# Finishing the output tiles from sums without the last two expert blocks

## What is computed

```
x = x + hier_moe(rmsnorm(x, norm2_g), w_rg, b_rg, w_re, b_re, w_gate, w_up, w_down)
y = rmsnorm(x, norm_f_g)

def hier_moe(x, ...):              # top-1 of 4 groups, then top-2 of the 4 experts in it
    for e in range(N_EXPERTS):     # 16 experts, d_model 1024, d_expert 512
        hid = jax.nn.silu(x @ w_gate[e]) * (x @ w_up[e])
        y = y + gates[..., e:e + 1] * (hid @ w_down[e])
```

## Time and profile before

| | |
|---|---|
| median of three runs | 938.05 us (937.69, 938.05, 940.88) |
| span of the profiled execution | 939.7 us, 1.65 us above the median; the page gives no other time for that execution |
| TensorE busy | 880.8 us, 94% |
| VectorE, ScalarE, GpSimd busy | 431.1, 154.5, 374.6 us |
| expert stage (first block's matmuls to the last's) | 534 to 908 us, 16 blocks |
| tail behind the last matmul | 908 to 939.7 us |
| granted clock of TensorE, mean | 0.976 |
| DMA | 163.15 MB, mean 174 GB/s, in the expert stage 291 to 360 GB/s a slice |

### The profile page before, as it was taken

One profiled execution on the slowest core, in us unless ns is written; L12 is line 12 of the kernel. 1 busy time (PEld: TensorE's weight loads), 2 busy tenths in 40 slices (PEclk: granted clock), 3 DMA queues, 4 the chain that ended last, 5 costly groups with the idle time before them and its releaser, 6 DMA issues.

```text
span 939.7 us, 16689 instructions
## 1 busy us (share of the span) xinstructions
PE 880.8 (94%) x6339; PEld 755.1 (80%) x6339; DVE 431.1 (46%) x1166; ACT 154.5 (16%) x456; POOL 374.6 (40%) x576
## 2 busy tenths in 40 slices
PE   5989999999999999999989799999999999999960
PEld 3974987869588695886945699999999999999920
DVE  3144474645646456463557843333333333333264
ACT  2031212121311213111131210000000000000071
POOL 4040031210302103021150258767767776777524
PEclk9989999999999999999999899999999999999985
DMA  9930203030110301003027389999999999999883
GB/s 328 280 151 1 68 1 80 12 79 1 28 52 1 79 1 34 25 1 57 1 62 291 71 294 299 327 352 335 360 346 333 327 322 326 315 319 314 248 305 115
DMA packets 90039, 163.15 MB, mean 174 GB/s; under 512 B 48887, under 2 KB 59027, under 8 KB 81770
## 3 DMA queue, kind: packets, MB, share of 16 engines
q1 hardware_dynamic: 70062, 136.43, 41.5%
q0 software_dynamic: 17728, 25.28, 11.2%
q10 hardware_dynamic: 2188, 0.59, 0.3%
HBM read 139.83 MB, written 25.87 MB: 176 GB/s over the span
## 4 chain that ended last, share of the span: by engine, by line
PE 51%; DMA 16%; issue 11%; POOL 11%; DVE 9%; ACT 1%; POOLq 1%; DVEq 0%; SPq 0%; ACTq 0%
PE bank L1527 48%; DMA z_d<-wout,win 12%; POOL z_d L599 7%; DVE wout L1443 2%; POOL wout L551 2%; PE bank L1532 1%; DVE wout L1436 1%; DVE win L1482 1%; DMA wout<-h_d,idt 1%; DMA h2T<-z_d 1%; DVE win L1407 1%; PE bank L1732 0%; DMA xbuf<-in_x_prompt 0%; POOL pad L595 0%; PE bank L1645 0%
## 5 line engine op out<-in xcount | busy, mean ns | idle before, releaser
L1527 PE MATMUL bank<-wout,win 128*128 128x150 f32 (+3 forms) x2048 | 246.3, 282 | 1.1 <-DVE wout L1129 1.1
L1527 PEld LDWEIGHTS bank<-wout,win 128*128 128x128 f32 x2048 | 244.7, 190 | 1.2 <-DVE wout L1129 1.2
L1527 PE MATMUL bank<-hT,win 128*128 128x128 f32 (+1 forms) x1536 | 182.9, 279 | 0.0
L1527 PEld LDWEIGHTS bank<-hT,win 128*128 128x128 f32 x1536 | 178.6, 192 | 1.5 <-issue 1.2
L1527 PE MATMUL bank<-win 128*128 128x130 f32 (+5 forms) x1024 | 137.3, 294 | 2.7 <-DVE win L1428 1.4
L599 POOL DMA_INDIRECT z_d<-wout,win x75 | 125.2, 1669 | 27.1 <-issue 26.8
L1527 PEld LDWEIGHTS bank<-win 128*128 128x128 f32 (+2 forms) x1024 | 125.5, 191 | 12.3 <-issue 10.3
L1527 PE MATMUL bank<-win,hT 128*128 128x260 f32 (+3 forms) x512 | 122.2, 417 | 3.0 <-DVE xbuf L1247 1.5
L1527 PE MATMUL bank<-wout,mixT 128*128 128x512 f32 (+1 forms) x384 | 116.8, 487 | 1.8 <-ACT mixT L845 1.7
L1527 PEld LDWEIGHTS bank<-win,hT 128*128 128x128 f32 (+1 forms) x512 | 77.1, 173 | 43.0 <-issue 34.1
L1436 DVE STREAM_TRANSPOSE wout<-bank 128x480 f32<-128x480 f32 (+1 forms) x45 | 25.1, 603 | 156.7 <-DMA z_d<-wout,win 155.2
(11 more groups left out here) (308 smaller groups left out, 812.0 us busy)
## 6 DMA issues: line engine op xcount, KB each, us to landing
win<-in_w_gate SPq DMA_DIRECT2D x32, 1024.0 KB, 6.3
win<-in_w_up SPq DMA_DIRECT2D x32, 1024.0 KB, 9.2
win<-in_w_down SPq DMA_DIRECT2D x32, 1024.0 KB, 10.6
win<-in_w_in SPq DMA_DIRECT2D x4, 2048.0 KB, 20.1
xbuf<-in_x_prompt SPq DMA_DIRECT2D x8, 512.0 KB, 3.8
wout<-in_w_out SPq DMA_DIRECT2D x1, 4096.0 KB, 15.6
z_d<-xbuf SPq DMA_DIRECT2D x32, 128.0 KB
h_d<-xn SPq DMA_DIRECT2D x8, 512.0 KB, 2.7
```

The lines of the kernel that those rows point to most:

```text
L1527: return nc.tensor.matmul(out, lhsT, rhs, start=first, stop=last)
```

## The change

The experts of positions 2 and 3 of the order (the smallest two beside experts 0 and 1) now get the last two positions, with blocks of 125 rows; the others move up. The kernel then finishes in this way:
- All nine tiles are read from `z_d` when the adds of block `sooner + 1` have landed, so their sums lack the last two blocks. Four tiles are read between the two halves of the last block's gate and up weights, five behind the second half. They are squared, normed and stored by SyncE.
- The adds of block `sooner + 2` still go to `z_d`, but wait until all nine tiles have been read (`sums_read`).
- Then the rows of both last blocks are read from `z_d` by two gathers of 125 rows (`fb`). Rows of the second last block need only the norm. Rows of the last block get its result added first. Both are written by indirect DMAs over the tiles, when these have landed.
- A row in both of the last blocks belongs to the last one. To leave it out of the other list, VectorE compares each id of the second last block with all ids of the last one (`lid`, loaded to all partitions), before it starts on block `sooner + 2`, and `away` moves such a row out of bounds.
- `products` of the last block stand behind the norms of both groups on VectorE, its silu behind all squares on ScalarE with a table load on either side. The last block's result has 8 products of 125 rows by 512 columns. `SHARED` is gone, the tiles `yb` lie in other buffers, and the gain `nfg` is loaded before block 3's weights.

```diff
-    SLOTS = ((30, 1), (30, 1), (26, 6), (27, 2), (28, 2), (30, 2))
+    SLOTS = ((30, 1), (30, 1), (26, 4), (27, 2), (28, 2), (30, 2))
     NS = sum(n for _, n in SLOTS)
-    SIZES = [NP * r for r, n in SLOTS for _ in range(n)] + [BLOCK] * (NE - NS)
+    LR, FX = 25, NE - 2
+    SIZES = [NP * r for r, n in SLOTS for _ in range(n)] + [BLOCK] * (FX - NS) + [NP * LR] * 2
...
+        order = sb("order", [P, NE])
...
+            after(sp, "stores", 16 * 8)
+            sp.dma_start(nfg, norm_f_g.rearrange("(a d) -> a d", a=1).broadcast_to([P, D])).then_inc(nf_in, 16)
             after(sp, "table_ready", 1)
             nblocks = sp.value_load(tabi[0:1, 2 * (NB + 1):2 * (NB + 1) + 1], min_val=NE, max_val=NB)
             sooner = sp.value_load(tabi[0:1, 2 * (NB + 1) + 1:2 * (NB + 1) + 2], min_val=NE - 3, max_val=NB - 3)
-            with sp.Fori(3, nblocks + 1) as j:
+            with sp.Fori(3, nblocks) as j:
...
+            def fetch_sums(t):
+                sp.dma_start(xa[t][0:ROWS[t], :], z_d[START[t]:START[t] + ROWS[t], :]).then_inc(z_rows[t], 16)
+            e = sp.value_load(tabi[0:1, bass.ds(nblocks - 1, 1)], min_val=0, max_val=NE - 1)
+            sp.wait_ge(gu_half, nblocks)
+            load_gate_up(e, 0)
+            sp.wait_ge(added, 16 * NP * (sooner + 1))
+            for t in GROUPS[0]:
+                fetch_sums(t)
+            sp.wait_ge(gu_done, 4 * nblocks)
+            load_gate_up(e, 1)
+            for t in GROUPS[1]:
+                fetch_sums(t)
+            sp.wait_ge(d0_used, nblocks)
+            load_down(e, 0)
+            sp.wait_ge(dn_done, 3 * nblocks)
+            load_down(e, 1)
             for t in range(NT):
-                sp.dma_start(xa[t][0:ROWS[t], :], z_d[START[t]:START[t] + ROWS[t], :]).then_inc(z_rows[t], 16)
-            after(sp, "stores", 16 * 8)
+                R = ROWS[t]
+                sp.wait_ge(yo_ready, t + 1)
+                dst = y_prompt[0, START[t]:START[t] + R, :] if t != DECP else y_sample[0, :, :]
+                sp.dma_start(dst, yb[t][0:R, :]).then_inc(y_out, 16)
+            sp.wait_ge(y_out, 16 * NT)
...
-            def add_block(k, r, n, first=False):
+            def add_block(k, r, n, first=False, sums_read=False):
...
+                if sums_read:
+                    for t in range(NT):
+                        pool.wait_ge(z_rows[t], 16)
...
-            last = row_of(nblocks)
-            pieces = ids_d[bass.ds(last, BLOCK), :].rearrange("(i a) n -> a i n", a=NP)
+            last, before = row_of(nblocks), row_of(sooner + 2)
+            pieces = ids_d[bass.ds(last, FN), :].rearrange("(i a) n -> a i n", a=NP)
+            pool.dma_start(lid.rearrange("p a n -> p (a n)"), ids_d[bass.ds(last, FN), :].rearrange("a n -> (a n)").unsqueeze(0).broadcast_to([P, 2 * FN])
+                           ).then_inc(lid_in, 16)
+            pool.dma_start(fid[0:FN, 1, :], ids_d[bass.ds(before, FN), :]).then_inc(lid_in, 16)
             for a in range(NP):
-                i, at = (0, a * RP) if a < NP - 1 else (1, 0)
-                pool.dma_start(fid[at:at + RP, i, :], pieces[a]).then_inc(fid_in, 16)
-            pool.wait_ge(carried, 7 * sooner + 13)
-            add_block(sooner + 2, RP, 7 * sooner + 13)
+                pool.dma_start(fid[a * LR:(a + 1) * LR, 0, :], pieces[a]).then_inc(fid_in, 16)
...
+            pool.wait_ge(away_ready, 1)
...
+            flink(g.tensor_tensor(fcol[:, :, 2], fcol[:, :, 2], away, ALU.add))
+            flink(g.tensor_tensor(fcol[:, :, 1], fcol[:, :, 0], away, ALU.add))
             flink(g.tensor_copy(frow, fcol))
+            pool.wait_ge(carried, 7 * sooner + 13)
+            add_block(sooner + 2, LR, 7 * sooner + 13, sums_read=True)
             pool.wait_ge(added, 16 * NP * (sooner + 2))
+            pool.wait_ge(carried, 7 * sooner + 17)
+            pool.wait_ge(fs0, 2)
             carry_wait()
-            for i, n in enumerate(FROWS):
-                g.indirect_dma_start(out=fb[i][0:n, :], out_offset=None, in_=z_d, in_offset=bass.IndirectOffsetOnAxis(
-                    ap=frow[0:n, i, 0:1].bitcast(U32), axis=0)).then_inc(base_in, 16)
-            for t in STORED:
-                R = ROWS[t]
-                if t in SHARED:
-                    at = t - SHARED[0] + 1
-                    pool.wait_ge(scaled, at)
-                    g.tensor_tensor(yb[t][0:R, :], yb[t][0:R, :], nfg[0:R, :], ALU.mult).then_inc(weighed, 1)
-                    pool.wait_ge(weighed, at)
-                else:
-                    pool.wait_ge(yo_ready, t + 1 - sum(1 for x in SHARED if x < t))
-                dst = y_prompt[0, START[t]:START[t] + R, :] if t != DECP else y_sample[0, :, :]
-                pool.dma_start(dst, yb[t][0:R, :]).then_inc(y_out, 16)
+            for i in (1, 0):
+                g.indirect_dma_start(out=fb[i][0:FN, :], out_offset=None, in_=z_d, in_offset=bass.IndirectOffsetOnAxis(
+                    ap=frow[0:FN, i, 0:1].bitcast(U32), axis=0)).then_inc(base_in, 16)
...
-            with act.Fori(NS + 1, nblocks + 1) as j:
+            sooner = act.value_load(tabi[0:1, 2 * (NB + 1) + 1:2 * (NB + 1) + 2], min_val=NE - 3, max_val=NB - 3)
+            with act.Fori(NS + 1, sooner + 2) as j:
                 expert(j, RP)
+            expert(sooner + 2, LR)
...
+                    link(a.activation(scrap[t % 2][0:R, :], xa[t][0:R, :], ACT.Square, accum_out=fs[0:R, 0, t:t + 1]))
+                start_norm(fs0, group[0], group[-1] + 1)
+            act.preload_act_table_set("silu_and_others")
+            expert(nblocks, LR)
+            act.preload_act_table_set("natural_log_exp_and_others")
+            act.wait_ge(base_in, 16 * 2)
+            link(a.activation(fy[1][0:FN, :], fb[1][0:FN, :], ACT.Square, accum_out=fs[0:FN, 0, NT + 1:NT + 2]))
+            start_norm(fs1, NT + 1, NT + 2)
...
+            a.activation(fy[0][0:FN, :].rearrange("p (m q i) -> p q m i", m=KD, q=NQ),
+                         fb[0][0:FN, :].rearrange("p (q m i) -> p q m i", m=KD, q=NQ), ACT.Copy).then_inc(base_ready, 1)
+            act.wait_ge(mixed, 1)
+            link(a.activation(fb[0][0:FN, :], fy[0][0:FN, :], ACT.Square, accum_out=fs[0:FN, 0, NT:NT + 1]))
+            start_norm(fs1, NT, NT + 1)
...
+            for r, count in SLOTS + ((RP, FX - NS), (LR, 2)):
                 n = NP * r
                 v.memset(szv[:, p0:p0 + count], float(n))
                 p0 += count
+            v.tensor_copy(order[:, 0:2], iof[:, 0:2])
+            v.tensor_copy(order[:, 2:FX], iof[:, 4:NE])
+            for n in range(2):
+                v.memset(order[:, FX + n:FX + n + 1], 3.0 - n)
...
+            link(v.tensor_copy(ends, ej[:, FX:NE]))
             link(v.tensor_reduce(out=ex, in_=tab[:, :, :], axis=AX.X, op=ALU.add))
+            link(v.tensor_scalar(more, ex, NE - 0.5, None, ALU.is_lt))
...
+            link(v.tensor_tensor(bx, bx, more, ALU.mult))
+            link(v.tensor_scalar(behind, jx, xin[0:1, NE - 1:NE], 0.5, ALU.subtract, ALU.is_ge))
+            link(v.tensor_tensor(rt[0:1, 62:63], ends[:, 1:2], ends[:, 0:1], ALU.subtract))
+            link(v.tensor_scalar(behind, behind, rt[0:1, 62:63], ends[:, 0:1], ALU.mult, ALU.add))
+            link(v.tensor_tensor(ex, ex, behind, ALU.subtract))
+            link(v.tensor_tensor(ex, ex, more, ALU.mult))
+            link(v.tensor_tensor(ex, ex, behind, ALU.add))
...
+            with dve.Fori(NS + 1, sooner + 2) as j:
+                block_of(j, RP)
...
+            dve.wait_ge(lid_in, 16 * 2)
+            link(v.memset(away, 0.0))
+            link(v.tensor_scalar(same, lid[:, :, 0], fid[:, 1, 0:1], float(4 * SEQ), ALU.is_equal, ALU.mult))
+            v.tensor_reduce(out=away[:, 1:2], in_=same, axis=AX.X, op=ALU.add).then_inc(away_ready, 1)
+            block_of(sooner + 2, LR)
             dve.wait_ge(nf_in, 16)
             norms(0)
+            outputs(GROUPS[0])
             norms(1)
+            products(nblocks, LR)
+            outputs(GROUPS[1])
+            dve.wait_ge(base_ready, 1)
+            for c in range(2):
+                cols = slice(c * (D // 2), (c + 1) * (D // 2))
+                dve.wait_ge(last_done, c + 1)
+                last = v.scalar_tensor_tensor(out=fy[0][0:FN, cols], in0=B[FBANK[c]][0:FN, :], scalar=fid[0:FN, 0, 1:2],
+                                              in1=fy[0][0:FN, cols], op0=ALU.mult, op1=ALU.add)
+            last.then_inc(mixed, 1)
             dve.wait_ge(fs1, 1)
+            rstd(NT + 1, NT + 2)
+            normed(fy[1], fb[1], FN, NT + 1).then_inc(fo_ready, 1)
+            dve.wait_ge(fs1, 2)
+            rstd(NT, NT + 1)
+            v.scalar_tensor_tensor(out=fy[0][0:FN, :], in0=fy[0][0:FN, :], scalar=fs[0:FN, 3, NT:NT + 1],
+                                   in1=nfg[0:FN, :], op0=ALU.mult, op1=ALU.mult).then_inc(fo_ready, 1)
...
-            with nc.Fori(NS + 1, nblocks, engines=PE_ONLY, head_slot=HEAD) as j:
```

(19 more changed lines are left out.)

124 lines of the change are left out of this document (41 added, 83 removed).

## The result

The change makes the kernel slower. The changed kernel takes **947.55 us**, the median of 4 runs (946.21 to 949.24), beside 939.46 for the kernel before (4 runs, 937.69 to 941.43): ratio 1.0084, 95% interval [1.0068, 1.0099]. The forecast was 931.0 in 926 to 943. The profiled execution has a span of 944.3 and its own time is 946.21.

A forecast was written before the change was run, and what follows sets the result against it. TensorE was taken to bound the expert stage, then the adds into z_d the tail. A loss of 13.6 us and a gain of 20.6 gave 7.0 less: 938.05 − 7.0 = 931.0 us, range 926 to 943.

The forecast's parts named there:

- What bounds the kernel: TensorE bounds the expert stage; from 880 only the chain of adds into z_d counts, with a 47.5 us tail.
- step 1: Block order and sizes: still 16 blocks, block 14 ends at 857.6; the order by itself gains nothing.
- Step 2: VectorE's list wait ahead of block 15: TensorE stands 5.6 us, half clock costs 3 more, gated rows ready at 889.7.
- Step 3: SyncE's queue of sums and weights behind block 14's adds: 20.6 us in all, all sums in at 893.6.
- Step 4: Block 15's adds wait for all sums, run 12.2 us from 893.6, land at 905.8: loses 13.6 us.
- Step 5: Tail behind block 15's adds: gathers land in 4.5 us, last scatters add nothing, end 932.7: wins 20.6 us.
- Rival B: Gathers and scatters of 125 rows spread over few of 16 DMA engines: 8 us more, 939; chance 0.28.
- Rival A: The whole kernel goes as the summed steps say: 931.0 us, own range 927 to 938; chance 0.50.
- C: Sums' reads on the path at 267 GB/s, block 15's adds landing 3 later, gathers at 9.2: 947; chance 0.11.
- D: TensorE and VectorE become the bound through a late list or lasting half clock: 935; chance 0.08.
- E: A seventeenth block, if a row count fails: 24.5 us more, 955; chance 0.03.

The follow-up runs named there:

- both: Changed kernel with 128 rows per gather and final scatter, and VectorE's list wait moved behind block 15's transpose, products and scaling: 944.0 us, ratio 1.0039.
- late_gap: late_outputs with VectorE's wait for the list put back ahead of block 15, as in the changed kernel: 940.53 us, ratio 1.0008.
- weights_first: late_outputs with SyncE loading the second gate and up weight half ahead of its wait for block 14's adds and the sums: 940.08 us, ratio 1.0005.
- late_outputs: both, with VectorE starting the last five tiles' outputs only when GpSimd has issued the two gathers: 937.67 us, ratio 0.997.
- rows128: Changed kernel with 128 rows instead of 125 in each gather and final scatter, the extra ones padding: 941.42 us, ratio 1.0006.
- sums_elsewhere: both, with the nine tiles read from h2_d instead of z_d and block 15's adds not waiting for these reads: 940.53 us, one run.

## Why the prediction was wrong

**What bounds the kernel, and step 1**: right. Block 15 starts at 857.3 by the prediction's clock (855.14 + 2.17), predicted 857.6.

**Step 2** (the list): right in kind, but not as harmless as the sum took it to be. The gap is 7.36 us instead of 5.6, since block 14's adds took 15.4 and not 13.2. TensorE's delay costs nearly nothing at the end: the last sum is in 361.2 us behind block 1's start with the gap and 361.1 without it (`both`). But the same wait puts the first four outputs of VectorE where they hold GpSimd's one-element operation, 2.5 us of it in the changed kernel and 3.3 in late_gap. The prediction has no term for that.

**Step 3** (SyncE's queue): right. The adds of block 14 are seen at 872.9 and the last sum at 893.3 in this profile, 20.4 us, predicted 20.6; both are late by what step 2 missed. Its picture, that the order of the queue sets this time, was not borne out: in weights_first another order left the time where it was.

**Step 4** failed. It said "So from 893.6, not from 889.7, the 12.2 us run". The 12.2 came from block 15's adds in the kernel before, where VectorE wrote no outputs and nothing was stored beside them. The change puts both there, and it became 16.8. The parts: 2.1 for the one-element operation held by VectorE (the first scatter is issued 2.9 behind its start instead of 0.8), 2.2 for the landing beside the stores (4.5 against 2.35), 0.2 in the issues. The first part comes from the first four outputs, the second from the stores of the last five. Step 5 even listed the latter, outputs from 902 to 910 and stores to 914, and counted them as done beside. That this is the cause is shown by the runs with 128 rows: late outputs bring the landing back (2.36 in late_gap), the first four outputs earlier bring the operation back to 0.18, and late_outputs, with both, takes 12.4.

**Step 5** failed in two terms. "I take 4.5, bounds 2.5 and 9" for the gathers' landing measured 6.7 (920.43 − 913.72), and 4.8 with 128 rows (918.43 − 913.64); the other 0.8 of the 3.0 are the dearer issues and the start. "So nothing is added" for the last scatters measured 4.6. That sentence called them "the same four scatters", which they are not: before they had 120 and 30 rows, now 125 and 125. Rival B named the cause, and its size of 8 is near the measured 3.0 + 4.6. Undoing it gave 6 to 7 back. I gave it 0.28 because no row of the trace moved 125 rows. But the rule that the prediction cites gives 5 engines for 125 rows (it stands in the section on the semaphore's 16, cited above, not in the one on queues), and nothing spoke for an even spread. With B as the likeliest case the forecast would have been 939; with steps 4 and 5 as measured it is 931.0 + 4.6 + 7.6 = 943, with the 1.9 of step 2 as well it is 945, and the kernel before is itself 1.4 higher in the runs beside the change than in the three shown (939.46 against 938.05). Rival A's own range was drawn too narrow: the bounds of its steps add up to 926 to 943, not 927 to 938.

**Rivals C and D**: C's size, 947, is near the result for other reasons; its reads at 267 GB/s didn't come (all sums in at 893.3), but its adds landing later did. D's gap came and was covered. E didn't come: 16 blocks.

**What stays open.** Three scatter issues lie beside VectorE's outputs in `both`; the third and fourth of the block take 1.58 and 1.66, and only the fifth 5.23; in the changed kernel two of them lie beside outputs and take 1.64 and 1.66. What decides which of them is held was not worked out. What property of the outputs holds GpSimd was not tried by itself. The 1.3 us that the final stretch is dearer than before with 128 rows (13.8 against 12.5) is not explained either. It is not the amount moved: in rows128 the DMA engines are idle from 932 to the end at 939.0.

## What to carry to other kernels

Count the rows of every DMA that a change resizes, and take a number with 16 as divisor, even if the extra rows are padding: 128 rows, the only such number tried, were 6 us faster than 125 here. When a change moves work of one engine beside a chain that was alone until then, the chain's duration from the old trace no longer holds; look for what VectorE runs beside GpSimd's short operations and issues, and for what is stored beside adds whose landing is waited for. An edit that takes a visible gap away can lose time, if what it brings forward lands on such a chain.

## What the runs showed of the hardware that was not expected

VectorE's operations that held GpSimd here all had two inputs in SBUF, and they held it for longer than one of them lasts. One row pair of late_outputs shows the plain case, a one-element operation of GpSimd that ends with VectorE's:

```profile
883.75 1.49 DVE L1495 TENSOR_TENSOR wout<-wout,win 128x1280 f32<-128x1280 f32 x1 [4.25 <-POOL win L645]
883.80 1.49 POOL L630 TENSOR_TENSOR pad<-pad 1x1 f32<-1x1 f32 x1
```

Beside a run of back-to-back outputs, operations of 0.4 us each, a one-element operation took 2.7 to 3.9 us and ended within 0.1 us of the run (in six of the kernels). The issue of an indirect DMA took 2.7, 4.4 and 5.2 us, and ended 1.4 to 1.5 us behind the run. But not every operation is caught: in rows128 the one at 893.62 took 0.32 in the middle of such a run (891.41 to 897.83), and it was the second scatter that was held. Beside VectorE's transpose (859.60 to 862.10 in late_outputs, one input) the first scatter's issue took its usual 1.65.

The Trainium skill (SBUF — State Buffer, Who interferes with whom) says that a VectorE instruction with two SBUF inputs contends with a GpSimd instruction that reads SBUF. Its rules for kernel authors on the same page add that the second of the two to issue is blocked until the first finishes. The traces agree that GpSimd is blocked (1.49 us above); here it could last longer than one instruction.

And block 15's adds, of 125 or 150 rows, have landed 2.2 to 2.5 us behind the end of the last issue when no tiles are stored beside them, and 3.3 to 5.95 us behind it when some are (6.9 with reads beside them too, in sums_elsewhere). Stores are not the only thing that can stand beside adds: block 14's, beside weights, landed some 5.6 us behind it in the kernel before (875.44 − 869.86).
